# Crossings of the second block done token tile by token tile

## The chip, the cores and the metric

One core of one Trainium2 chip runs the whole program. The metric is the device time of one execution in microseconds (us); three executions of the kernel before are given, and one more was recorded by the hardware profiler. Engines: PE is TensorE, DVE VectorE, ACT ScalarE, POOL GpSimd, SP SyncE (it issues DMAs).

## What is computed

Two transformer blocks follow each other, each of two layers, on 256 tokens of 1024 features in float32. The change touches the second block (layers 2 and 3 of the program). Cut to what matters there:

```
for each layer of block 2:
    g1, s1, gate1, g2, s2, gate2 = rows and columns of c @ w_ada + b_ada
    h = rmsnorm(x) * (1 + g1) * g_attn + s1          # 256 x 1024
    q, k, v of three kinds of attention = h @ w_in   # 13 weight tiles
    y = attention(...)                               # 256 x 1024
    x = x + gate1 * (y @ w_out)                      # 4 weight tiles
    h = rmsnorm(x) * (1 + g2) * g_ffn + s2
    layer 2:  x = x + gate2 * ((silu(h @ w_gate) * (h @ w_up)) @ w_down)   # 11 steps of 256 hidden columns
    layer 3:  a router picks 2 of 8 experts for each token; x = x + gate2 * their sum
```

## The kernel before

Tokens are two tiles of 128 (`TT = 2`, index `t`), features eight chunks of 128 (`KC = 8`, index `k`), output columns two halves of 512 (index `c`). All large products are made of three: weights and left sides are each split in a high part (`w_hi`, `hT_hi`, rounded by ACT) and a low part (`w_lo`, `hT_lo`, the rest, by DVE or POOL), and `product` (L2379 to L2383) multiplies high by high, high by low and low by high. So every weight tile of 128 x 2048 goes through: DMA into a raw slot of `slab` (SP, L648), the high part on ACT (`hi`, L1920, about 1.9 us), the low part on DVE (`lo`, L999, 2.29 us) or on POOL in four pieces (L848), and products on PE. `Tiles` numbers the tiles and their raw and split slots, and `POOLED` says which low parts POOL makes. PE waits for a low part in `next_low`, and releases a split slot with `w_used`. Every engine works through its own program in order; the order of tiles and waits is written out by hand.

A *crossing* is what lies between the last products of a stage and the first of the next. In block 2 there are four: into layer 2 from block 1 (whose last layer ends with the modulation's rows, L2820), from layer 2's output tiles to its gated stage, from its down tiles to layer 3, and from layer 3's output tiles to the router. The last three are `cross_gated` (L1098 on): DVE adds the four parts (c, t) to `x`, gated (`add_gated`, L1095 and L1096), in the order (0,0), (0,1), (1,0), (1,1); ACT squares each half row (`square_halves`, L1951), DVE makes the mean (L1105, L1110), POOL the root (`norm_roots`, L828), DVE scales the row into `h` (L1118). PE turns all 16 chunks (`turn_rows`, L2392), with `tp_done` raised only at token tile 1. `turn` then takes the chunks one by one, 256 tokens wide: DVE applies gain and shift out of PSUM into `htf` (L1039), ACT rounds to `hT_hi` (L1985), DVE takes the rest to `hT_lo` (L1034). PE waits with `rows_one` for each chunk and uses it for both token tiles at once.

Around the crossings: `out_tile(2, FA)` does both token tiles of output half 0, then `out_last` half 1. POOL makes the low parts of the first two gate/up tiles, and roots between their pieces (`ff_lo`); SP loads the next gate/up tile only after both (`pool_lo(FF0[l] + 1)`). In a gated step ACT does silu (L2247) and then the high parts of the next tiles; DVE does the gate product (L598), then low parts, then the hidden low part (L1587); PE turns the hidden rows (`turn_step`, L2500). The last step is `down` for the tile before the last, with `turn_step(J - 1)` in its middle, then `down_last`. In layers 2 and 3 POOL makes tile 2's low part (`lo_of(l, 2)`) and ACT its high part before the turning (`hi_of(l, 2, 3)`). In layer 3 the router's products (`wr_hi`) take each chunk of `hT`, then PE turns all of `htf` for the rows that are gathered, and DVE copies the logits out (`lgT`, L1693).

## Time and profile before

| what | value |
| --- | --- |
| device time, median of 3 runs (lowest, highest) | 1903.46 us (1903.06, 1904.87) |
| profiled execution, its time | 1903.16 us |
| profiled execution, its span | 1901.4 us |
| PE busy | 1812.2 us, 95% |
| DVE busy | 1413.7 us, 74% |
| ACT busy | 1115.0 us, 59% |
| POOL busy | 385.0 us, 20% |
| mean granted PE clock | 0.981 |

All times in the rows are us from the start of the span. A row of a timeline has the start, the duration, the engine, the line, the operation with its output and inputs, the number of merged instructions, and in brackets how long the engine stood idle before it and what released it. The busy time of PE is modelled from its matmuls, which overlap, so 95% does not mean that it multiplies at its peak. The granted clock of 1.00 is 2.4 GHz, of 0.50 1.2 GHz.

### The profile page before, as it was taken

Reading aid. Unit: us, or ns where it says so; the run is one execution under the profiler, and the core shown is the slowest. Engines: PE = TensorE matmul, PEld = TensorE weight load, DVE = VectorE, ACT = ScalarE, POOL = GpSimd, SP = SyncE. Lnnn points to the kernel's source line nnn. Section 1 sums busy time; section 2 is a strip of 40 time slices with the busy share of each in tenths; the row PEclk is TensorE's granted clock in tenths of the full one; section 3 lists DMA queues with packets and bytes.
Section 4 is the critical chain, followed back from the end, with each engine's and each line's share of the span. In section 5 each row is a group of like instructions: output and inputs, shape, how many; then the busy total and the mean of one; then the engine's idle time right before and its main releaser. Section 6 shows DMA issues by size and latency. Waiting matters only on the chain.

```text
span 1901.4 us, 25928 instructions
## 1 busy us (share of the span) xinstructions
PE 1812.2 (95%) x8751; PEld 1476.9 (78%) x8751; DVE 1413.7 (74%) x1655; ACT 1115.0 (59%) x1296; POOL 385.0 (20%) x315
## 2 busy tenths in 40 slices
PE   7899999989999998899989789999999999999997
PEld 6678886868888786688878568888888888888885
DVE  5748874466976486645457759888988888889897
ACT  6745444564444454443345537777777777777775
POOL 3732213462211373200046400000000000000000
PEclk9999999999999998999989989999999999999999
DMA  8348884418987341455544249999999999999994
GB/s 271 111 167 330 333 348 149 143 58 302 361 331 290 105 156 45 155 189 186 193 155 144 100 178 352 384 378 386 376 384 381 380 381 380 380 377 382 384 381 166
DMA packets 237934, 506.39 MB, mean 266 GB/s; under 512 B 23304, under 2 KB 74720, under 8 KB 231712
## 3 DMA queue, kind: packets, MB, share of 16 engines
q1 hardware_dynamic: 225664, 492.85, 71.2%
q0 software_dynamic: 3008, 10.32, 2.0%
q10 hardware_dynamic: 9184, 2.23, 0.5%
q8 instruction: 43, 0.70, 0.2%
q14 instruction: 35, 0.29, 0.0%
HBM read 497.42 MB, written 7.91 MB: 266 GB/s over the span
## 4 chain that ended last, share of the span: by engine, by line
PE 83%; issue 6%; DVE 5%; ACT 4%; POOL 1%; DMA 0%; POOLq 0%; SPq 0%; DVEq 0%; ACTq 0%
PE bank L2381 26%; PE bank L2383 25%; PE bank L2382 25%; PE bank L2500 2%; ACT slab L2070 1%; ACT w_hi L1920 1%; PE bank L2820 1%; DVE slab L1317 1%; PE bank L2592 1%; PE bank L2569 1%; POOL w_lo L848 1%; PE bank L2551 0%; PE bank L2537 0%; DVE x L1096 0%; PE bank L2603 0%
## 5 line engine op out<-in xcount | busy, mean ns | idle before, releaser
L999 DVE TENSOR_TENSOR w_lo<-slab,w_hi 128x2048 fp32r<-128x2048 f32 x369 | 848.0, 2309 | 213.1 <-ACT w_hi L1920 212.5
L1920 ACT ACTIVATE w_hi<-slab 128x2048 fp32r<-128x2048 f32 (+2 forms) x421 | 796.6, 1899 | 326.3 <-PE bank L2383 251.5
L2381 PE MATMUL bank<-w_hi,hT_hi 128*128 128x512 f32 (+3 forms) x1664 | 648.7, 390 | 15.3 <-DVE hT_lo L1048 4.5
L2382 PE MATMUL bank<-w_lo,hT_hi 128*128 128x512 f32 (+3 forms) x1664 | 637.5, 383 | 0.0
L2383 PE MATMUL bank<-w_hi,hT_lo 128*128 128x512 f32 (+3 forms) x1664 | 637.5, 383 | 0.0
L2381 PEld LDWEIGHTS bank<-w_hi,hT_hi 128*128 128x128 f32 x1664 | 315.7, 190 | 77.3 <-DVE w_lo L999 8.8
L2383 PEld LDWEIGHTS bank<-w_hi,hT_lo 128*128 128x128 f32 x1664 | 315.3, 189 | 59.5
L2382 PEld LDWEIGHTS bank<-w_lo,hT_hi 128*128 128x128 f32 x1664 | 316.0, 190 | 55.2
L848 POOL TENSOR_TENSOR w_lo<-slab,w_hi 128x512 fp32r<-128x512 f32 (+2 forms) x208 | 256.0, 1268 | 375.7 <-ACT w_hi L1920 358.8
L2381 PE MATMUL bank<-w_hi,hid_hi 128*128 128x512 f32 x680 | 265.6, 391 | 0.7 <-DVE w_lo L999 0.7
L2383 PE MATMUL bank<-w_hi,hid_lo 128*128 128x512 f32 x680 | 264.9, 390 | 0.0
L2382 PE MATMUL bank<-w_lo,hid_hi 128*128 128x512 f32 x680 | 264.6, 389 | 0.0
L2381 PEld LDWEIGHTS bank<-w_hi,hid_hi 128*128 128x128 f32 x680 | 127.7, 188 | 29.3 <-issue 2.3
L2383 PEld LDWEIGHTS bank<-w_hi,hid_lo 128*128 128x128 f32 x680 | 127.6, 188 | 26.7
L2382 PEld LDWEIGHTS bank<-w_lo,hid_hi 128*128 128x128 f32 x680 | 127.7, 188 | 26.1
L946 POOL DMA_INDIRECT y_rows<-slab,posi x7 | 16.5, 2363 | 515.6 <-ACT slab L2293 515.6
L923 POOL TENSOR_TENSOR slab<-slab 128x512 f32<-128x512 f32 x32 | 58.9, 1858 | 252.8 <-ACT slab L2218 252.8
L1605 DVE SCALAR_TENSOR_TENSOR big<-slab,csilu,big 128x2048 f32<-128x2048 f32 x42 | 103.5, 2473 | 0.0
L2070 ACT ACTIVATE slab<-slab,att 128x256 f32<-128x256 f32 (+1 forms) x144 | 67.1, 469 | 48.8 <-DVE att L1293 39.7
L2209 ACT ACTIVATE hid_hi<-bank 128x512 fp32r<-128x512 f32 (+1 forms) x95 | 47.6, 528 | 46.1 <-PE bank L2500 46.1
L1587 DVE TENSOR_TENSOR hid_lo<-bank,hid_hi 128x512 fp32r<-128x512 f32 (+1 forms) x95 | 55.3, 603 | 0.0
L2569 PE MATMUL bank<-const,slab 128*128 128x128 f32 x224 | 35.7, 298 | 19.7 <-DVE slab L1317 13.1
(253 smaller groups left out, 1199.7 us busy)
## 6 DMA issues: line engine op xcount, KB each, us to landing
slab<-in_w_exp_gate SPq DMA_DIRECT2D x176, 512.0 KB, 7.0
slab<-in_w_exp_up SPq DMA_DIRECT2D x176, 512.0 KB, 7.4
slab<-in_w_exp_down SPq DMA_DIRECT2D x176, 512.0 KB, 7.0
slab<-in_w_ada SPq DMA_DIRECT2D x48, 1024.0 KB, 6.1
slab<-in_w_mlp_in SPq DMA_DIRECT2D x64, 512.0 KB, 6.2
slab<-in_w_mlp_out SPq DMA_DIRECT2D x64, 512.0 KB, 9.0
slab<-in_w_in SPq DMA_DIRECT2D x56, 512.0 KB, 5.1
slab<-in_w_out SPq DMA_DIRECT2D x32, 512.0 KB, 4.6
```

The costliest lines, as they stand in the source:

```text
L848: ins = pool.tensor_tensor(w_lo[:, q, o], raw(s)[:, o], w_hi[:, q, o].bitcast(F32), ALU.subtract)
L923: pool.tensor_tensor(scr(X_ACT2 + t * F_UP, F_UP), a, a, ALU.mult).then_inc(sq_done, 1)
L999: dve.tensor_tensor(w_lo[:, q, 0:n], raw(s)[:, 0:n], w_hi[:, q, 0:n].bitcast(F32), ALU.subtract).then_inc(lo_dve, 1)
L1587: dve.tensor_tensor(to_lo[:, f0:f0 + n, o], src, to_hi[:, f0:f0 + n, o].bitcast(F32), ALU.subtract).then_inc(hidl_done, 1)
L1605: ins = dve.scalar_tensor_tensor(acc, w, c, acc, ALU.mult, ALU.add)
L1920: act.activation(w_hi[:, q, 0:n], raw(s)[:, 0:n], ACT.Copy).then_inc(hi_done, 1)
L2070: act.activation(p, p, ACT.Exp, bias=att[:, 1, j, t:t + 1], scale=-1.0, accum_out=att[:, 2, j, t:t + 1]).then_inc(ex_done, 1)
L2209: act.activation(to_hi[:, f0:f0 + n, t * P:(t + 1) * P], src, ACT.Copy).then_inc(hidh_done, 1)
L2381: pe.matmul(dst, a_hi, b_hi, start=start, stop=False)
L2382: pe.matmul(dst, a_hi, b_lo, start=False, stop=False)
L2383: return pe.matmul(dst, a_lo, b_hi, start=False, stop=stop_)
L2569: ins = pe.transpose(bank[PT[s]][:, o:o + P], sp_row(l, s, u, t)[:, k * P:(k + 1) * P], ident)
```

## The change

In block 2 all work at the crossings is ordered by token tile. `cross_gated` adds (0,0), (1,0), (0,1), (1,1) as (c, t); ACT, not DVE, scales a row; `turn(t, b)` treats half the chunks of one token tile: four 128-column evacuations on DVE, then ACT's and DVE's parts for two chunks at a time. With `late`, DVE adds (1,1) before turning token tile 0, else after its first half. PE's new routines `out_by_token`, `in_tiles_by_token`, `up_by_token`, `next_up` and `down_by_token` hold two weight tiles and go through token tile 0 first, with `turn_row` of a token tile placed inside. The modulation gains of a layer (`mod_gains`) are computed ahead of the crossing. POOL makes its roots after both `ff_lo`. Tile 2's low part moves from POOL to DVE (`BY_DVE2`). In layer 3 ACT's `hi_of(l, 2, 3)` comes after `cross_gated`. The split slots of the gated stage start at 3, those of layer 3's tiles at 2, so that the first two gate/up tiles need not wait for the last output tiles. The gated stage's first silu is done per token tile. The diff, cut to its core:

```diff
@@ constants
+FF_SLOT, LAST_SLOT = 3, 2
-        BY_DVE1, BY_DVE2 = range(2, 6), range(3, 5)
+        BY_DVE1, BY_DVE2 = range(2, 6), range(2, 5)
-        ATT2_BANKS, FF2_BANKS = (6, 7, 2, 3), (2, 3, 4, 5)
+        ATT2_BANKS, FF2_BANKS = {DEPTH: (1, 2, 3, 7), DEPTH + 1: (0, 1, 2, 3)}, (2, 3, 4, 6)
@@ POOL
                     norm_roots()
-                    lo_of(l, 2)
                     lo_of(l, 5, 6, 7, 8, 9, 10, 11, 12, 13, 14)
...
                     if l < MOE:
-                        ff_lo(l, 0, norm_roots)
+                        ff_lo(l, 0)
                         ff_lo(l, 1)
-                    else:
-                        norm_roots()
+                    norm_roots()
@@ DVE
+            def turn(t, b, l, which):
+
+                m, o, at = turn_at(l, which), slice(t * P, (t + 1) * P), pairs_turned(l, which, t, b)
+                dve.wait_ge(tp_done, turns_before(m) + 2 * t + b + 1)
+                for i in range(2):
+                    for k in range(4 * b + 2 * i, 4 * b + 2 * i + 2):
+                        ins = dve.tensor_scalar(htf[:, k, o], turned_row(l, which, k, t), turn_gain(l, which, k), turn_shift(l, which, k),
+                                                ALU.mult, ALU.add)
+                    ins.then_inc(tpe_done, 1)
+                for i in range(2):
+                    ks = slice(4 * b + 2 * i, 4 * b + 2 * i + 2)
+                    dve.wait_ge(hh_done, splits_before(2 * DEPTH) + at + i + 1)
+                    dve.tensor_tensor(hT_lo[:, ks, o], htf[:, ks, o], hT_hi[:, ks, o].bitcast(F32), ALU.subtract).then_inc(hl_done, 1)
...
                 add(0, 0)
+                first_half(0)
+                add(1, 0)
+                mean(0)
                 add(0, 1)
...
                 if late:
                     add(1, 1)
+                    first_half(1)
+                    turn(0, 0, l, which)
                     mean(1)
+                    turn(0, 1, l, which)
                 else:
+                    first_half(1)
+                    turn(0, 0, l, which)
                     add(1, 1)
+                    turn(0, 1, l, which)
                     mean(1)
+                turn(1, 0, l, which)
+                turn(1, 1, l, which)
...
-                    cross_gated(add_last, l < MOE)
+                    cross_gated(add_last, l == MOE, l, 1)
@@ ACT
+            def cross_gated(late, l, which):
+
+                square_part(0, 0)
+                square_part(1, 0)
+                scaled_row(0, l, which)
+                square_part(0, 1)
+                turn(0, 0, l, which)
+                if late:
+                    square_part(1, 1)
+                    turn(0, 1, l, which)
+                else:
+                    turn(0, 1, l, which)
+                    square_part(1, 1)
+                scaled_row(1, l, which)
+                turn(1, 0, l, which)
+                turn(1, 1, l, which)
...
                 elif l > DEPTH:
-                    square_halves()
+                    cross_gated(True, l, 0)
                     hi_of(l, 2, 3)
-                    turn()
...
                     hi()
-                    if l == MOE:
-                        hi()
+                    hi()
@@ PE
+                def out_by_token():
+
+                    q = [next_low(), next_low()]
+                    for t in range(TT):
+                        for c in range(2):
+                            for k in range(4):
+                                if t and c and k == 2:
+                                    turn_row(0, l, 1)
...
+                def in_tiles_by_token():
...
+                        if not t and l > DEPTH:
+                            turn_row(1, l, 0)
...
+                    def up_by_token():
...
+                                if not t and k == 6:
+                                    turn_row(1, l, 1)
...
+                    def next_up():
+
+                        q = next_low()
+                        for t in range(TT):
+                            pe.wait_ge(sq_done, ub + t + 1)
+                            if t:
+                                turn_step(0)
...
+                    def down_by_token(at):
+
+                        pe.wait_ge(hidl_done, at + TT)
+                        before_last, last = next_low(), next_low()
...
+                        part(0, 0, before_last, False)
+                        part(0, 1, before_last, False)
+                        turn_step(J - 1)
+                        part(1, 0, before_last, False)
+                        pe.wait_ge(hidl_done, at + 2 * TT)
+                        part(0, 0, last, True).then_inc(part_done, 1)
+                        part(0, 1, last, True).then_inc(part_done, 1)
+                        part(1, 1, before_last, False).then_inc(w_used, 1)
+                        part(1, 0, last, True).then_inc(part_done, 1)
+                        part(1, 1, last, True).then_inc(w_used, 1)
+                        turn_row(0, l + 1, 0)
...
                 for t in range(TT):
+                    if t:
+                        turn_row(1, l, 1)
+                    for k in range(KC):
+                        if k % 2 == 0:
+                            split_pair(l, 1, t, k)
+                        ins = product(bank[5][0:NE, t * P:(t + 1) * P], wr_hi[:, k, :], wr_lo[:, k, :], *lhs(k, t), k == 0, k == KC - 1)
+                    if t:
+                        ins.then_inc(lgt_done, 1)
                     for k in range(KC):
                         ins = pe.transpose(bank[2 * t + k // 4][:, (k % 4) * P:(k % 4 + 1) * P], htf[:, k, t * P:(t + 1) * P], ident)
```

## Rows read from the trace of the kernel before

**Rows 1.** Stretches, gated loop: busy us (count) of PE, PEld, DVE, ACT, POOL; clock.

```profile
800.00:950.00 150.00, 150.00 (x680) 124.16 (x679) 74.03 (x63) 59.62 (x62) 0.00 (x0) 1.00 0.59 193
```

**Rows 2.** PE's timeline, layer 2's output tiles to gated stage: start, duration, idle before.

```profile
772.46 1.09 PE L2392 MATMUL bank<-const,h 128*128 128x128 f32 x8 [3.59 <-DVE h L1118]
...
777.39 0.77 PE L2381 MATMUL bank<-w_hi,hT_hi 128*128 128x512 f32 x1 [0.77 <-DVE hT_lo L1034]
...
777.95 0.63 PE L2382 MATMUL bank<-w_lo,hT_hi 128*128 128x512 f32 x1
...
778.38 0.63 PE L2383 MATMUL bank<-w_hi,hT_lo 128*128 128x512 f32 x1
...
791.15 0.77 PE L2500 MATMUL bank<-const,slab 128*128 128x128 f32 x4 [0.93 <-DVE slab L598]
```

**Rows 3.** Timeline of DVE, the same crossing.

```profile
763.54 0.69 DVE L1095 TENSOR_TENSOR slab<-bank,rowg 128x512 f32<-128x512 f32 x1 [10.33 <-PE bank L2383]
...
764.27 0.69 DVE L1096 TENSOR_TENSOR x<-slab,x 128x512 f32<-128x512 f32 x1
...
777.17 0.53 DVE L1039 TENSOR_SCALAR slab<-bank,modg,modcol 128x256 f32<-128x256 f32 x1
...
777.62 1.03 DVE L1034 TENSOR_TENSOR hT_lo<-slab,hT_hi 128x256 fp32r<-128x256 f32 x1
...
781.24 0.41 DVE L1034 TENSOR_TENSOR hT_lo<-slab,hT_hi 128x256 fp32r<-128x256 f32 x1
```

**Rows 4.** Timelines of ACT and POOL, the same crossing.

```profile
765.36 0.61 ACT L1951 ACTIVATE h<-x 128x512 f32<-128x512 f32 x1
...
770.95 0.54 POOL L828 TENSOR_TENSOR stat<-stat,half 128x1 f32<-128x1 f32 x1 [0.75 <-DVE stat L1110]
```

**Rows 5.** Groups by form (count, busy us, mean ns); ACT's timeline entering layer 2.

```profile
L1293 DVE CUSTOM_DVE_ANT_0 slab<-bank,const 128x256 f32<-128x256 f32 x60 | 23.3, 417 | 28.0 <-PE bank L2551 28.0
...
L1293 DVE CUSTOM_DVE_ANT_0 slab<-bank,const 128x128 f32<-128x128 f32 x28 | 8.0, 285 | 4.6 <-PE bank L2551 4.5
...
631.65 1.06 ACT L1942 ACTIVATE h<-x 128x1024 f32<-128x1024 f32 x1
```

**Rows 6.** Timelines of POOL and SP's queue, same crossing.

```profile
772.78 7.01 POOL L848 TENSOR_TENSOR w_lo<-slab,w_hi 128x512 fp32r<-128x512 f32 x5
...
780.13 0.38 SPq L648 DMA_DIRECT2D slab<-in_w_ff_gate  x1
```

**Rows 7.** Timelines of ACT and DVE at layer 2's last gated step.

```profile
954.11 0.66 ACT L2247 ACTIVATE slab<-bank 128x256 f32<-128x256 f32 x2 [8.91 <-PE bank L2383]
...
954.66 1.92 ACT L1920 ACTIVATE w_hi<-slab 128x2048 fp32r<-128x2048 f32 x1
...
956.61 2.29 DVE L999 TENSOR_TENSOR w_lo<-slab,w_hi 128x2048 fp32r<-128x2048 f32 x1 [1.33 <-ACT w_hi L1920]
```

**Rows 8.** Timelines of PE and ACT, down tiles of layer 2 to layer 3.

```profile
969.42 2.82 PE L2392 MATMUL bank<-const,h 128*128 128x128 f32 x12 [3.96 <-DVE h L1118]
...
968.37 3.69 ACT L1920 ACTIVATE w_hi<-slab 128x2048 fp32r<-128x2048 f32 x2
...
983.93 0.78 ACT L2047 ACTIVATE big<-bank 128x324 f32<-128x324 f32 x2 [4.02 <-PE bank L2383]
```

**Rows 9.** Stretches with the granted clock behind POOL's columns, same crossing.

```profile
968.00:970.00 2.00, 0.58 (x3) 0.58 (x4) 1.07 (x3) 2.00 (x3) 1.43 (x2) 0.67 1.08 358
...
978.00:980.00 2.00, 2.00 (x12) 2.00 (x12) 1.84 (x6) 1.17 (x3) 0.00 (x0) 0.77 0.67 251
```

**Rows 10.** Timelines of PE and POOL, entering layer 2.

```profile
647.38 0.40 PE L2381 MATMUL bank<-w_hi,hT_hi 128*128 128x512 f32 x1
...
634.68 5.02 POOL L848 TENSOR_TENSOR w_lo<-slab,w_hi 128x512 fp32r<-128x512 f32 x4 [0.60 <-ACT w_hi L1920]
```

**Rows 11.** Timelines of PE and DVE, layer 3's output tiles to router.

```profile
1108.06 1.47 PE L2392 MATMUL bank<-const,h 128*128 128x128 f32 x8 [2.17 <-DVE h L1118]
...
1117.90 0.41 DVE L1693 COPY slab<-bank 8x256 f32<-8x256 f32 x1 [0.61 <-PE bank L2383]
```

More of the change, by code:

```diff
@@ L169, in before_split @@
         if not self.looping and self.i - self.at < self.split:
-            return self.last.get(self.base + self.i % self.split)
+            return self.last.get(self.slot(self.i))
         return self.t - self.split
@@ L461, in splits_before, with turns_before, turn_at @@
             return 4 * min(m, 2 * DEPTH) + KC * max(0, m - 2 * DEPTH)
+        def turns_before(m):
+            return KC * min(m, 2 * DEPTH) + 4 * max(0, m - 2 * DEPTH)
+        def turn_at(l, which):
+            return 2 * DEPTH + 2 * (l - DEPTH) + which
+        PART0 = {l: PARTS * l if l < DEPTH else PARTS * DEPTH + 5 * (l - DEPTH) for l in LAYERS}
         def att_slot(k):
@@ L755, in _ @@
                     ff_end = ring.t
-                    ring.stage(RAW)
+                    ring.stage(RAW, base=LAST_SLOT)
                 else:
@@ L1243, in _ @@
                     norm()
+                    mod_gains(0)
+                    for t in range(TT):
+                        turn(t, 0, l, 0)
+                        turn(t, 1, l, 0)
                     ada_rows(l - 1)
[L1245 to L1250 removed]
                 if l == 0:
@@ L2795, in read_by_act @@
                         pe.wait_ge(act_done, ub + t + 1)
-                    up(rows_to, left, TT, COL, mlp_rows if l < DEPTH else rows_one)
+                    def up_by_token():
+                        q = []
+                        for t in range(TT):
+                            for k in range(KC):
+                                a, s = k // 4, slice(k % 4 * COL, (k % 4 + 1) * COL)
+                                if k % 4 == 0:
+                                    if not t:
+                                        q.append(next_low())
+                                if k % 2 == 0:
+                                    split_pair(l, 1, t, k)
+                                if not t and k == 6:
+                                    turn_row(1, l, 1)
+                                ins = product(rows_to[t][:, :], *lhs(k, t), w_hi[:, q[a], s], w_lo[:, q[a], s], k == 0, k == KC - 1)
+                                if t and k % 4 == 3:
+                                    ins.then_inc(w_used, 1)
+                            if not t:
+                                ins.then_inc(row_half, 1)
@@ new lines, in down_by_token, with part @@
+                    def down_by_token(at):
+                        pe.wait_ge(hidl_done, at + TT)
+                        before_last, last = next_low(), next_low()
+                        def part(t, c, q, spare):
+                            o = slice(t * P, (t + 1) * P)
+                            for f in range(2):
+                                s = slice(f * D + c * COL, f * D + (c + 1) * COL)
+                                f_hi, f_lo = hidden(f, ROWS_SPARE if spare else None)
+                                ins = product(sums_at(t, c), f_hi[:, o], f_lo[:, o], w_hi[:, q, s], w_lo[:, q, s], False, spare and f == 1)
+                            return ins
+                        part(0, 0, before_last, False)
[9 more added lines that the diff above has]
+                        turn_row(0, l + 1, 0)
```

240 lines of the change are left out of this document (126 added, 114 removed).

## The prediction

> **What bounds the kernel now.** Read first the page, where TensorE (PE) has by far the most busy time, then the table of stretches: in the gated loop of layer 2 PE is busy for all 150.00 us with 680 matmuls, 0.221 us each [rows 1]. A delay or gain before such a loop reaches the end undiminished. What this change can touch are PE's holes at the four crossings of block 2, so the timelines there come next, PE's first (a hole shows as "idle before"), then VectorE's (DVE), ScalarE's (ACT) and GpSimd's (POOL) for what fills it. I call them X1 (into layer 2), X2 (its output tiles to its gated stage), X3 (its down tiles to layer 3), X4 (layer 3's output tiles to the router).
>
> At X2 PE stops at 772.46 - 3.59 = 768.87, turns token tile 0, waits, turns tile 1, waits 0.77, and multiplies from 777.39 at a pitch of 0.43 (777.95 to 778.38) instead of 0.22; its first hidden transposes come at 791.15 [rows 2]. Meanwhile DVE works almost without a break [rows 3].
>
> **Prices.** A gated addition is two DVE instructions of 0.69, 1.34 in all; evacuating one 256-column chunk starts 0.45 before the next instruction (777.17 to 777.62); a low part is 0.41, but 1.03 while POOL splits weights [rows 3]. The square of half a row is 0.61, some 0.8 with the read of its sum, and POOL's root 0.54 [rows 4]. The halved evacuation (128 columns, two pointer scalars) isn't in the trace. The masked maximum takes 0.417 for 256 and 0.285 for 128 columns [rows 5], so 128 columns are worth 0.13: 0.45 - 0.13 = 0.32 a piece. The bound from below is the 0.285 row less the overlap of 0.08 (0.53 - 0.45), 0.21; from above 0.45. I take 0.32, since it is the same operation with its width alone changed. One token-and-half group `turn(t, b)` is then 4 x 0.32 + 0.1 + the wait for ACT's second high part + 2 x 0.38, about 2.2; four of them 8.8, against 8 x (0.45 + 0.34) = 6.3 for today's eight chunks. Scaling a row goes from DVE to ACT, where 1024 columns took 1.06 [rows 5]. Today's chunk of 256 columns takes 0.53 from start to end [rows 3]. The Trainium skill (VectorE: DVE Perf Modes, the section on the TRN2 errata) gives an instruction from PSUM 120 cycles fixed and one per element, an estimate of 0.39 for the chunk and 0.26 for a piece; the trace does not agree, and the measurement decides. By the page's figure a group is about 0.25 shorter and each crossing 1 us; the sum would come out some 3 lower.
>
> **X2, the gain.** Output tiles 2 and 3 are four sets of 12 matmuls, 2.7 each. They started at 768.87 - 10.9 = 758.0 and end sets at 760.7, 763.4, 766.2 (and 768.9). Tile 0's additions now come after the first two, so: add 760.8 to 762.2, square to 763.0, add 763.5 to 765.0, square 765.8, mean 766.05, root 766.7, row scaled by ACT 767.9. PE wants it at 767.5 inside its last set: 0.4 idle. Transposes (1.0) and rest end 770.4. DVE is held by `first_half(1)`, whose square is behind the row scaling on ACT, to 768.9; group (0,0) ends 771.1, its first pair is ready at 770.8. DVE then adds the last part (to 772.5) and does group (0,1): pair 2 at 774.3, PE idle 0.8. PE then needs token tile 1 turned after pair 2, at 775.7. Its row is behind ACT's last high part (774.35), the square (775.2), mean, root (776.1) and scaling (777.2): 1.6 idle. From 777.3 PE has the 8 transposes, 6 matmuls, 24 for token tile 1: 785.1. The second pair of gate/up tiles is loaded earlier: POOL's two splits no longer end at 779.8 (772.78 + 7.01), which is what SyncE waited for before loading at 780.13 [rows 6], but at 765, as both use free slots. Its high part still stands behind ACT's turns (to 781.8): high 783.7, low 786.1, gate product 786.5: PE waits 1.4, then ends those tiles at 786.5 + 10.9 + 0.5 = 797.9. Before: 791.15 + 0.77 + 10.9 = 802.8. **Gain 4.9.** The slow low parts (1.03 against 0.41) go with POOL's splits. If PE's clock falls in these holes, half a slow stretch, up to 3.4, is lost again: bounds 1.5 to 5.5.
>
> **X3, a loss.** `down_by_token` takes both split tiles before its first product: `before_last, last = next_low(), next_low()`. Before, PE needed only the earlier one at this point. The last down tile's split stands behind the last gate step: silu 954.11, high part from 954.66, low part 956.61 to 958.90 [rows 7]. PE is ready at 953.9 and would wait to 958.9: **5.0 idle** where 12 matmuls ran. The rest of the 48 matmuls and the four transposes is as long as before, so the down tiles end at 970.4, not 965.46 (969.42 - 3.96 [rows 8]). All DVE, ACT and POOL work behind is later too. Chain from the first finished part: add 965.1 to 966.5, square, add to 969.0, square, mean 970.05, root, scale 971.9; transposes; additions of tile 1 hold DVE to 972.9; groups (0,0) to 975.1; the second square of tile 1 stands before ACT's next high parts, so mean 975.9, (0,1) to 977.9; row 1 scaled by 978.7; PE turns it at 979.3 to 980.3; (1,0) to 982.0, (1,1) to 984.1. Then comes the next one: `hi_of(l, 2, 3)` moves behind ACT's turns. Before, it ran at 968.37 in the hole [rows 8]. And tile 2's low part moves from POOL to DVE, behind its turns. High part 983.9 to 985.8, low 988.1. PE waits there, where it went straight on at 983.9 (ACT reads the finished tiles at 983.93 [rows 8]). **Loss 4.2** at a full clock. But today's 3.96 idle was followed by a granted clock of 0.67 in 968 to 970, then the lower level (1.2 GHz), until 0.77 in 978 to 980 [rows 9], which puts the slow stretch at 968.7 to 978.9. A 5.0 idle should do the same over 957 to 964: 5 us of half speed in the down tiles, 2.5 later, of which 2.3 reach the chain. **Loss 6.5**, bounds 2.4 (cheap pieces, clock kept) to 9 (a second slow stretch in tiles 0 and 1).
>
> **X1, a small loss.** The transposes start as before, behind other PE work. The first pair is ready 1 us earlier, but DVE's four groups take 8.8: 637.3 to 646.1, then `ada_rows` 0.65, then tile 2's low part 2.3: 649.1. PE began tile 2 at 647.38, as POOL had made this low part by 634.68 + 5.02 [rows 10]. **Loss 1.8**, bounds 0 (cheap pieces) to 2.5.
>
> **X4, a loss.** PE stopped at 1105.9 (1108.06 - 2.17); the logits left it for DVE's copy at 1117.90 [rows 11]. After: parts at 1097.8, 1100.5, 1103.2; row 0 scaled 1104.9; transposes push the last set to 1107.25. Here `late` is true: DVE's last addition waits for it before any turning, to 1108.7. Groups (0,0) to 1111.0; ACT's square after its high parts, mean 1111.7; (0,1) to 1113.8; row 1 scaled 1114.6. PE: router products to 1114.4, eight transposes of `htf` at the slow pitch of X3's (2.82 for 12, so 0.23 each [rows 8]) to 1116.2, only then `turn_row(1)`. Four are done at 1117.1: (1,0) to 1119.4, (1,1) to 1121.5, logits copied at about 1121.5 to 1122. The other copies on ACT end before the selection needs them. **Loss 3.6**, bounds 1.5 to 4.5.
>
> **Sum.** 1.8 - 4.9 + 6.5 + 3.6 = +7.0 us. The profiled execution took 1903.16 (span 1901.4); the median shown is 1903.46, 0.3 above. 1903.46 + 7.0 = 1910.5.
>
> **The rivals.**
> - *Pieces are cheap (not slower).* At a pitch of 0.21 each group of four is 0.45 shorter, 1.8 in each of X1, X3, X4 and 0.5 in X2: +7.0 - 5.9 = +1.1, 1904.6. For: the 0.285 row. Against: today's chunk takes 0.53 where that operation takes 0.417. At 0.27 it is about +4 still; below that it decides. 0.17. The Trainium skill's figure above (VectorE: DVE Perf Modes, an estimate of 0.26 a piece from start to end) lies on this side.
> - *The clock holds.* No slow stretch in X3 (-2.3) and X4 (-1.4): +3.3, 1906.8. For: 0.93 idle at 791.15 was followed by no slow matmuls. Against: 5.0 is longer than the 3.59 and 3.96 that were [rows 2, 8]. 0.17.
> - *Overlap everywhere.* If each crossing gave X2's 4.9, X3's waits being covered (another order on DVE than the code has), and X1 nothing: about -14, 1889. Against: DVE's unbroken work. 0.08.
> - *Clock falls in X2 as well and twice in X3*: +3.4 + 2.5 and 1 in X1: +14, 1917. 0.10.
>
> **How the numbers follow.** My case 0.48. Range 1900.5 to 1916.5: cheap pieces with the clock kept below, most of the last rival above, leaving out overlap everywhere. A measurement here tells about 0.2% (3.8 us) from no change. Faster 0.10 (overlap 0.08, tail of cheap pieces); same 0.27 (cheap pieces 0.14, clock 0.10, 0.03 of mine); slower 0.63.
>
> **What would show it.** X2: PE's hole of 3.59 gone, the table load and silu at about 785, hidden transposes at about 789. X3: PE idle about 5 ended by DVE's low part ahead of the first down product; a second hole ended by a low part ahead of tile 2; the span of 12 matmuls slow after it. X1: DVE's split between `ada_rows` and tile 2's products. X4: `lgT` copied 3 to 4 later after PE's last output matmul. DVE's 128-column evacuations at 0.40 long. Wrong if the down tiles start at once, or if pieces are near 0.28.

## The result and the profile after

The changed kernel is slower than the kernel before, by more than was forecast and beyond the range.

| what | before | after |
| --- | --- | --- |
| device time, median | 1903.65 us (4 runs) | 1922.28 us (4 runs, 1921.09 to 1923.44) |
| ratio, 95% interval | | 1.0098 (1.0086 to 1.0110) |
| profiled execution: time, span | 1903.16, 1901.4 us | 1921.96, 1919.8 us |
| mean granted PE clock | 0.981 | 0.978 |

The page of the kernel after, its busy times: PE does 5.6 us more in 18.4 us more span, so most of the loss is waiting.

```profile
PE 1817.8 (95%) x8775; PEld 1481.0 (77%) x8775; DVE 1423.2 (74%) x1683; ACT 1121.3 (58%) x1302; POOL 377.0 (20%) x307
```

**Where it is.** I took the same PE instruction in both traces at seven places and subtracted the two distances between neighbouring places. Predicted terms stand beside what came out (us, after less before; at the last place after is 18.7 behind, the sum but for rounding):

| stretch | predicted | measured |
| --- | --- | --- |
| the program's start to the first transposes of layer 2 (code untouched) | 0 | +1.3 |
| X1, and on to 700 us | +1.8 | +2.7 |
| attention of layer 2 | 0 | +0.4 |
| X2 | -4.9 | -4.0 |
| X3 | +6.5 | +10.6 |
| attention of layer 3 | 0 | +0.2 |
| X4, to the first expert's products | +3.6 | +7.6 |

PE's timeline of after at X2. It answers to [rows 2]: the hole of 3.59 is one of 1.45, the eight transposes of the second row take 1.06 at a full clock, and ahead of the next gate/up pair PE waits 1.14 for DVE (1.4 forecast).

```profile
773.34 1.09 PE L2439 MATMUL bank<-const,h 128*128 128x128 f32 x8 [1.45 <-ACT h L2012]
...
782.26 1.06 PE L2439 MATMUL bank<-const,h 128*128 128x128 f32 x8 [1.15 <-ACT h L2012]
...
791.55 0.47 PE L2430 MATMUL bank<-w_hi,hT_hi 128*128 128x512 f32 x1 [1.14 <-DVE slab L629]
```

A part of X2's gain may be PE's clock. Before has a stretch at the lower level over its transposes and first products here, and after has none. Two stretches of the same kind as in [rows 1], first of before, then of after:

```profile
774.00:781.00 7.00, 5.58 (x17) 4.47 (x18) 6.18 (x11) 2.08 (x5) 5.79 (x5) 0.51 0.01 2
```

```profile
773.00:781.00 8.00, 7.01 (x32) 5.10 (x32) 5.82 (x16) 3.21 (x10) 0.54 (x1) 1.00 0.99 348
```

How much of the gain the new order would bring by itself, at the same clock, no run tells.

DVE's timeline of after at X1. Four pieces take 1.36 to 1.37, and groups follow each other in 2.19 (640.89 to 643.08): 0.32 a piece and 2.2 a group, as priced. Behind them stands tile 2's low part, at 648.05, and PE's first product of tile 2 comes at 650.38, against 647.38 before [rows 10]; 1.26 of that was there before X1. The rest of X1's +2.7, 0.9, comes between tile 2 and 700 us.

```profile
640.89 1.36 DVE L1060 TENSOR_SCALAR slab<-bank,modg,modcol 128x128 f32<-128x128 f32 x4
...
643.08 1.36 DVE L1060 TENSOR_SCALAR slab<-bank,modg,modcol 128x128 f32<-128x128 f32 x4
...
648.05 4.47 DVE L1026 TENSOR_TENSOR w_lo<-slab,w_hi 128x2048 fp32r<-128x2048 f32 x2
```

PE's timeline of after at X3, to be read beside [rows 8]. The first line is the hole of `next_low()` ahead of the down tiles (5.0 forecast); the last is tile 2, 2.20 behind DVE's low part. Between them PE turns the second row at 984.14.

```profile
959.39 0.72 PE L2430 MATMUL bank<-w_hi,hid_hi 128*128 128x512 f32 x1 [4.96 <-DVE w_lo L1026]
...
975.54 1.09 PE L2439 MATMUL bank<-const,h 128*128 128x128 f32 x8 [2.91 <-ACT h L2012]
...
978.17 0.61 PE L2430 MATMUL bank<-w_hi,hT_hi 128*128 128x324 f32 x1 [1.53 <-DVE hT_lo L1066]
...
984.14 1.04 PE L2439 MATMUL bank<-const,h 128*128 128x128 f32 x8
...
992.97 0.50 PE L2430 MATMUL bank<-w_hi,hT_hi 128*128 128x512 f32 x1 [2.20 <-DVE w_lo L1026]
```

Stretches of after (busy us and counts of PE, PEld, DVE, ACT, POOL, then the granted clock, DMA share, GB/s). Three fall in X3, behind its holes: the first behind 4.96, the second behind 2.91 and 1.53, the third behind 2.20. One of over 20 us covers X4's second half and most of the gather. Before, X3 had one at 968 to 979 [rows 9].

```profile
959.00:964.00 5.00, 4.61 (x14) 3.68 (x15) 0.25 (x1) 0.00 (x0) 0.00 (x0) 0.66 0.73 245
976.00:984.00 8.00, 6.47 (x30) 6.26 (x29) 4.52 (x14) 3.43 (x9) 0.54 (x1) 0.57 0.19 70
993.00:997.00 4.00, 4.00 (x11) 3.15 (x12) 3.90 (x7) 3.21 (x3) 0.71 (x1) 0.57 0.74 228
1124.00:1146.00 22.00, 16.33 (x92) 15.01 (x93) 13.59 (x40) 5.54 (x12) 0.06 (x1) 0.50 0.41 152
```

PE's and then DVE's timeline of after at X4. PE has holes of 3.31 and 1.48; then the eight transposes of `htf` (L2977) and only then the second row (L2439), each 1.91 at the lower level; DVE waits 3.52 for that row. The gather takes 6.40, in before 5.44. The logits are copied 15.9 later than before [rows 11], 4.8 of it new since the entry of X4.

```profile
1121.73 0.23 PE L2430 MATMUL bank<-hT_hi,wr_hi 128*8 128x128 f32 x1 [3.31 <-DVE hT_lo L1066]
...
1124.31 0.27 PE L2430 MATMUL bank<-hT_hi,wr_hi 128*8 128x128 f32 x1 [1.48 <-DVE hT_lo L1066]
...
1125.55 1.91 PE L2977 MATMUL bank<-const,slab 128*128 128x128 f32 x8
...
1127.26 1.91 PE L2439 MATMUL bank<-const,h 128*128 128x128 f32 x8
...
1141.75 6.40 PE L2997 MATMUL bank<-slab,h 128*128 128x128 f32 x32 [1.37 <-DVE slab L1744]
```

```profile
1128.35 1.37 DVE L1060 TENSOR_SCALAR slab<-bank,modg,modcol 128x128 f32<-128x128 f32 x4 [3.52 <-PE bank L2439]
...
1133.78 0.41 DVE L1709 COPY slab<-bank 8x256 f32<-8x256 f32 x1 [0.97 <-PE bank L2432]
```

### The profile page after: what moved, and what is told of

Same layout as the page of the kernel before. It is cut to its first block, busy times and chain, and to the rows that moved or that the text cites. A ratio compares the mean times of both kernels' runs of the same rounds, so it can differ in the third digit from the quotient of the medians.

```text
span 1919.8 us, 26002 instructions
## 1 busy us (share of the span) xinstructions
PE 1817.8 (95%) x8775; PEld 1481.0 (77%) x8775; DVE 1423.2 (74%) x1683; ACT 1121.3 (58%) x1302; POOL 377.0 (20%) x307
## 4 chain that ended last, share of the span: by engine, by line
PE 80%; DVE 6%; issue 6%; ACT 5%; POOL 1%; DMA 1%; SPq 0%; POOLq 0%; DVEq 0%; ACTq 0%
PE bank L2430 24%; PE bank L2432 24%; PE bank L2431 24%; PE bank L2546 2%; ACT w_hi L1936 1%; ACT slab L2116 1%; PE bank L2959 1%; DVE slab L1060 1%; DVE slab L1335 1%; POOL w_lo L877 1%; PE bank L2639 1%; DVE w_lo L1026 1%; PE bank L2616 1%; DMA slab<-in_w_router 1%; PE bank L2598 0%
## 5 line engine op out<-in xcount | busy, mean ns | idle before, releaser
L877 POOL TENSOR_TENSOR w_lo<-slab,w_hi 128x512 fp32r<-128x512 f32 (+2 forms) x200 | 247.4, 1272 | 383.7 <-ACT w_hi L1936 366.8
```

Of the source, the lines that this page charges most:

```text
L877: ins = pool.tensor_tensor(w_lo[:, q, o], raw(s)[:, o], w_hi[:, q, o].bitcast(F32), ALU.subtract)
```

## The experiments

My theory was that the four crossings carry all of the loss, each by its own holes and by the slow clock (the lower level, 1.2 GHz) behind them. The rivals were a cost in what the change alters outside the crossings, and a shift that sets the stages against each other. Behind each time stand its ratio to the kernel before, measured beside it on the same chip, and the 95% interval; 0.001 is 1.9 us. "By the ratios" compares two kernels by these, which is fairer than their times where they ran on different chips.

**One crossing at a time.** For each crossing the order of before was put behind a switch: whole rows on DVE, ACT and PE, the old order of additions, the old output and down tiles. `WHOLE` lists (0, 0), (0, 1), (1, 0), (1, 1) for X1 to X4.

```diff
+WHOLE = {(0, 0), (0, 1), (1, 0), (1, 1)}
...
-                    cross_gated(add_last, l == MOE, l, 1)
+                    if whole(l, 1):
+                        cross_whole(add_last, l < MOE, l, 1)
+                    else:
+                        cross_gated(add_last, l == MOE, l, 1)
```

All four whole: 

> The changed kernel with all four crossings put back into the whole-row manner of before; kept of the change are the slot numbering of the weight tiles, tile 2's low part on VectorE, the gains worked out ahead, and the order of the roots on GpSimd. If the added time is all in the four crossings (my theory), this is before within 1.5 us: 1903 to 1905. If a part of it sits in what is kept (rival: tile 2's low part on VectorE and the slot order), it is 1906 or more. The start of the second block (first transposes, 636.67 before, 637.93 after) should be 636.7 if the 1.3 us of block 1 come from the crossings' code and 637.9 if they come from what is kept or from how things happen to fall.

Measured 1905.86 (1.0011, 1.0000 to 1.0023), between theory and rival. The first transposes of layer 2 come at 635.98 here and at 637.99 with X2 alone, so the 1.3 us of block 1 follow neither the crossings' code nor what is kept: they vary from one execution to the next. The first transposes of X2 come at 780.90, 10.42 idle, against 772.46 in before [rows 2], since POOL splits two gate/up tiles ahead of the roots that a whole-row X2 waits for, and the second waits for ScalarE. POOL's timeline of it:

```profile
774.64 4.92 POOL L892 TENSOR_TENSOR w_lo<-slab,w_hi 128x512 fp32r<-128x512 f32 x4 [13.37 <-ACT w_hi L2018]
779.52 1.36 POOL L874 TENSOR_TENSOR stat<-stat,half 128x1 f32<-128x1 f32 x2
```

So it is no clean zero: this order belongs to X2, and costs nothing only where X2 goes by token tile. With before's order of the roots:

```diff
-                        ff_lo(l, 0)
+                        ff_lo(l, 0, norm_roots if whole(l, 1) else None)
```

> As the kernel with all four crossings whole, with X2's roots on GpSimd put ahead of the last quarter of the first gated tile's low part, as before has them. The trace of the first such kernel shows its X2 transposes 6.2 us later than before's, behind the two low parts on GpSimd. Theory: that order is the whole of what it lost in X2, about 5 us, and what is left of the change outside its crossings (slots, tile 2's low part on VectorE) costs under 1.5 us: with the clock's stretch in X3 short (3.4 us, as in that kernel) 1899 to 1902, with before's long one (10.2 us) 1902 to 1905. Rival: the kept part costs something of its own: 1906 or more.

Measured 1900.91 (0.9988, 0.9979 to 0.9997), as the theory had it. On balance nothing outside the crossings costs anything: it gains 2.3 us by the ratio. The trace shows 0.8 lost in X1, where tile 2's low part is now on VectorE, and X3 2.7 shorter than in before. VectorE's low parts in it are no longer slowed by POOL splitting tile 2 beside them (first before, then this kernel), which is 1.1 by the next product, and the other 1.6 come while PE's clock is still low in before (10.2 us at the lower level there, 3.4 in this kernel).

```profile
972.96 1.48 DVE L1034 TENSOR_TENSOR hT_lo<-slab,hT_hi 128x256 fp32r<-128x256 f32 x1
```

```profile
972.89 0.42 DVE L1092 TENSOR_TENSOR hT_lo<-slab,hT_hi 128x256 fp32r<-128x256 f32 x1
```

This kernel, *all whole*, is the zero of the table below.

X2 alone: 

> Only X2 by token tile, the other three crossings whole. Theory: X2 alone gains what the trace of after shows between its ends, 4.0 us, and hands it on: about 1899.5 (1898.5 to 1901). Rival: the gain is taken back in the gated stage or in layer 3, then 1903 or more.

Measured 1898.68 (0.9970, 0.9957 to 0.9982): the theory.

X3 alone: 

> Only X3 by token tile. Theory: 8 to 9 us slower than the kernel without it (the trace of after has 8.6 between its ends, the prediction had 6.5), some 1911 to 1913, half of it in TensorE's 5 us hole ahead of the last down tiles and the rest at the lower clock level in the holes behind it. Rival: it costs only the 4.2 us of the first hole, since most of the slow clock was there before: 1908.

Measured 1918.16 (1.0073, 1.0060 to 1.0087), more than theory or rival.

X4 alone: 

> Only X4 by token tile. Theory: 4.9 us between its ends and 2.7 behind it, where gather and first expert run at the lower clock level in after: 1910 to 1911.5. Rival: what is behind it belongs to X3's shift and not to X4: 1908 to 1908.7, with the first expert's silu at most 5 us late.

Measured 1912.68 (1.0050, 1.0036 to 1.0063). X3 alone and X4 alone still have the late roots of the first kernel, so they are 0.0062 and 0.0039 over that one: 11.8 and 7.4 us. X4's 7.4 is the 7.6 of the theory, on a higher base. X3's 8 to 9 were too low: they were read against before, whose own X3 is 2.7 longer than the whole-row one kept here.

X1 put back: 

> The changed kernel with X1 alone put back. Theory: X1 is 1.5 to 2.5 us of the change (the piecewise order on VectorE ahead of layer 2's first tiles), so 1919.5 to 1921 against 1922.3 of after. Rival: X1 shifts attention of layer 2 against GpSimd's low parts and the 1.4 us added there are its work too: 1917 to 1919.

Measured 1920.32 (1.0083, 1.0069 to 1.0097), 2 us under after (2.9 by the ratios), with intervals that overlap. In the trace X1 is 2.0 shorter and the attention behind it 2.6 longer, so what X1 is worth at the end isn't settled.

What each kernel takes in a stretch over *all whole*, from the same PE instructions as above (us):

| kernel | X1 | attention 2 | X2 | X3 | X4 |
| --- | --- | --- | --- | --- | --- |
| before | -0.8 | 0.0 | +0.2 | +2.7 | 0.0 |
| after | +1.9 | +0.4 | -3.8 | +13.3 | +7.6 |
| X2 alone | 0.0 | +1.2 | -3.8 | +1.1 | +0.1 |
| X3 alone | -0.1 | +1.4 | (+4.5) | +13.1 | +0.1 |
| X4 alone | -0.1 | +1.4 | (+4.5) | 0.0 | +7.2 |
| X1 put back | -0.2 | +3.0 | -3.8 | +13.0 | +7.6 |
| late take | +2.0 | +0.9 | -3.8 | +7.1 | +7.6 |
| late take, early high parts | +2.3 | +0.5 | -3.8 | +3.8 | +7.3 |
| all edits | +1.9 | +0.5 | -3.8 | +3.7 | +3.5 |
| all edits, high parts split | +1.8 | +0.6 | -3.8 | +1.7 | +3.2 |

The crossings add up: each costs the same alone and together (X3 13.1 and 13.3, X4 7.2 and 7.6, X2 -3.8 in every kernel). That settles the rival of a shift for them; it isn't settled for X1 and the attention behind it, which goes from 0.4 to 3.0. The 4.5 in brackets are the late roots.

**X3's holes.** The late take:

```diff
-                        before_last, last = next_low(), next_low()
+                        before_last = next_low()
...
                         pe.wait_ge(hidl_done, at + 2 * TT)
+                        last = next_low()
                         part(0, 0, last, True).then_inc(part_done, 1)
```

> The changed kernel with one line moved: TensorE takes the last down tile (waits for its low part) only before its first product, no longer before those of the tile ahead of it. Theory: the 5.0 us hole ahead of the down tiles in X3 is that wait and nothing else, and one stretch at the lower clock goes with it (3.4 us of stretch, 1.5 of time): 1916 to 1918. Rival 1: the hole's time is only moved, TensorE waits later for the same low part or for the hidden rows: 1920 or more. Rival 2: the stretches at the lower clock are set by the later holes and stay: 1917.5 to 1918.5, clock stretches in X3 unchanged.

Measured 1916.17 (1.0062, 1.0048 to 1.0076), the theory: 6.1 under after (6.9 by the ratios), and 6.2 less between X3's ends. The hole is gone, and the slow stretch behind it:

```profile
952.00:960.00 8.00, 7.01 (x34) 5.48 (x33) 4.08 (x7) 5.46 (x7) 1.71 (x3) 1.00 0.08 12
```

Added to it, the early high parts:

```diff
                 scaled_row(1, l, which)
+                between()
                 turn(1, 0, l, which)
                 turn(1, 1, l, which)
...
-                    cross_gated(True, l, 0)
-                    hi_of(l, 2, 3)
+                    cross_gated(True, l, 0, lambda: hi_of(l, 2, 3))
```

> As the late take, and ScalarE makes the high parts of layer 3's tiles 2 and 3 right after the second scaled row, where it stands idle 3.8 us, no longer behind the last transposed pieces. Theory: the 2.2 us hole at tile 2 shrinks by the 1.6 us by which VectorE's low part waits for the high one, and its stretch at the lower clock (3.4) may go with it: 1.5 to 3.5 us below the late take. Rival: VectorE is what ends last there, and the pieces behind the high parts come later by as much: within 1 us of the late take.

Measured 1911.85 (1.0042, 1.0028 to 1.0056), 4.3 under the late take, more than the theory's 1.5 to 3.5: PE's wait ahead of tile 2 falls from 2.22 to 0.73, and the third slow stretch goes. So two orderings made 9.5 of X3's 13.3.

**X4: order and clock.** The second row first:

```diff
-                    if t:
-                        turn_row(1, l, 1)
                     for k in range(KC):
...
                     if t:
                         ins.then_inc(lgt_done, 1)
+                    else:
+                        turn_row(1, l, 1)
                     for k in range(KC):
                         ins = pe.transpose(bank[2 * t + k // 4][:, (k % 4) * P:(k % 4 + 1) * P], htf[:, k, t * P:(t + 1) * P], ident)
```

> Only X4 by token tile, and in it TensorE turns the second scaled row right behind the first token tile's router products, ahead of the eight transposes of the first tile's htf that stand there in the change. In the trace of X4 alone VectorE waits 3.52 us for that row's transposes, which TensorE issues only behind those eight (1.91 us at the lower clock level). Theory: this place in TensorE's order costs 1.7 us: 1910.5 to 1911.5 against 1912.7. Rival: what counts is the sum on TensorE up to the gather, the order inside it is all the same: within 0.5 us of 1912.7.

Measured 1910.01 (1.0038, 1.0023 to 1.0053), 2.3 under X4 alone by the ratios. In the trace X4 gets 3.7 shorter, more than the 1.7 of the order, and it spends less time at the lower clock level: 17.1 us from 1112 to 1140, against 23.9 from 1114 to 1145 in X4 alone.

The clock, by transposes of a constant in PE's two holes:

```diff
                     for k in range(KC):
+                        for _ in range({0: 26, 4: 10}.get(k, 0) if not t else 0):
+                            pe.transpose(bank[0][:, 0:P], ident, ident)
                         if k % 2 == 0:
                             split_pair(l, 1, t, k)
```

> Only X4 by token tile, and TensorE fills its 3.3 us hole ahead of the first router products with 26 transposes of the identity into a bank that is free, and the 1.5 us hole ahead of the fifth with 10; their results are used by nothing. They need 2.8 and 1.1 us at full clock, so they end before what they wait for. Theory: the lower clock comes from these holes, so the stretch at 1114 to 1121 goes or comes later, and the time falls by 1.7 to 3.5 us: 1909 to 1911. If the longer stretch of 1124 to 1139 goes with it, up to 6: 1906.5. Rival: the stretches are not set by these holes: 1912.2 to 1914, the fillers at most 0.5 us in the way.

Measured 1908.98 (1.0032, 1.0021 to 1.0044), 3.4 under X4 alone by the ratios, 3.5 shorter in the trace: the theory. First X4 alone, then the kernel with fillers, the same stretch:

```profile
1114.00:1121.00 7.00, 4.88 (x29) 4.41 (x28) 3.33 (x11) 2.34 (x5) 1.25 (x2) 0.51 0.56 225
```

```profile
1114.00:1121.00 7.00, 4.83 (x49) 3.78 (x47) 4.77 (x16) 2.96 (x6) 1.10 (x2) 1.00 0.56 225
```

PE's timeline of the kernel with fillers: 26 transposes fill the hole to 0.47, and the eight transposes behind take 1.04, not 1.91.

```profile
1109.30 3.00 PE L3112 MATMUL bank<-const 128*128 128x128 f32 x26
...
1112.77 0.23 PE L2530 MATMUL bank<-hT_hi,wr_hi 128*8 128x128 f32 x1 [0.47 <-DVE hT_lo L1081]
...
1116.29 1.04 PE L3119 MATMUL bank<-const,slab 128*128 128x128 f32 x8
...
1117.16 1.04 PE L2539 MATMUL bank<-const,h 128*128 128x128 f32 x8
```

No other edit was made, so PE's clock falls here by the crossing's own holes, and half of X4's loss (3.5 of 7.2) went with the fillers. Not all slow time went: of 23.9 us at the lower level from 1114 on in X4 alone 10.2 are left, from 1127 to 1141, over the gather and the first expert. The Trainium skill (TensorE: Matmul & The Clock Gate, the section on HAM oscillation) describes a matmul kernel in which each wait is followed by work at the lower clock; these rows agree, in that filling the waits takes the lower clock away from the transposes behind them.

Both edits (with 9 transposes in the second hole): 

> Only X4 by token tile, with both edits: the second row turned first and the fillers in the holes. Alone they gave 2.7 and 3.7 us of X4's 7.4. Theory: the first works largely through the transposes at the lower clock level, so they overlap by about 1 us: 5 to 5.8 us together, 1907 to 1907.7. Rival: they add up, 1906.2 or less; or the fillers do all of it, 1909.

Measured 1908.38 (1.0023, 1.0013 to 1.0033), 5.1 under X4 alone by the ratios, 4.1 in the trace. They overlap more than the theory had it, in the trace by 3.0 of 7.1: each takes away the same slow transposes. What is left of X4 in the trace, 3.1 us, was not taken apart.

**What is left of X3.** TensorE's order first:

```diff
+                                if not t and l > DEPTH and k0 + k == 6:
+                                    turn_row(1, l, 0)
...
-                        if not t and l > DEPTH:
-                            turn_row(1, l, 0)
```

> The late take and early high parts, and in layer 3 TensorE turns the second scaled row ahead of the last two chunks of tile 1's products of the first token tile, no longer behind them. In the trace of those two edits VectorE waits 3.44 us for that row's transposes (976.3) though the row was scaled by 974.1. Theory: X3's remaining cost is this place in TensorE's order, as in X4: 1.5 to 2 us below the 1911.9 of the two edits, 1909.9 to 1910.4. Rival: VectorE's pieces, 8.8 us for both token tiles, bound X3 whatever TensorE's order: 1911.4 or more.

Measured 1911.91 (1.0037, 1.0023 to 1.0052): the rival. X3 is 0.4 shorter in the trace.

The clock; `filler(n, to)` issues n transposes of the identity into a bank that is free:

```diff
+                        filler(18, bank[3][:, 3 * P:4 * P])
                         turn_row(0, l + 1, 0)
...
                     q = []
+                    if l > DEPTH:
+                        filler(11, bank[3][:, 3 * P:4 * P])
```

> The late take and early high parts, with 18 transposes of the identity in TensorE's 2.1 us hole ahead of layer 3's first transposes and 11 in the 1.4 us hole behind them. Theory: the stretch at the lower clock at 968 to 976 (6.8 us) comes from these holes; with it gone 2 to 3.5 us below 1911.9: 1908.5 to 1910. If the shift also shortens the 13.6 us stretch in X4, 1906. Rival: the stretch is set by the products' own holes behind (1.4 and 1.5 us) or just moves: within 0.7 of 1911.9.

Measured 1910.30 (1.0033, 1.0022 to 1.0044), below the two edits alone by less than the intervals tell apart. Its trace decides against the theory: PE's clock stays up in 968 to 976 (0.57 there with the two edits alone), yet X3 is as long (3.7 against 3.8). PE only waits longer, 2.54 against 1.36, for VectorE, and behind this hole comes a new stretch at the lower level, 3.4 us from 980.6. Without it X3 could be only some 0.5 shorter: tile 2's low part, which VectorE makes behind its pieces, is ready at 985.12, and PE's first product of tile 2 comes at 985.65.

```profile
968.00:976.00 8.00, 6.89 (x53) 6.22 (x52) 6.85 (x18) 5.06 (x11) 1.00 (x2) 1.00 0.54 179
```

```profile
980.45 0.53 PE L2430 MATMUL bank<-w_hi,hT_hi 128*128 128x324 f32 x1 [2.54 <-DVE hT_lo L1066]
```

All edits together: 

> All four crossings by token tile, with every edit tried so far: late take, early high parts, earlier second row in X3 and X4, fillers in the holes of X3 and X4. Theory: they add up: 1911.9 less 1.8 (order in X3), 2.5 (fillers in X3), 2.7 (order in X4) and 3 (fillers in X4, part of it gone with the order) is 1902, within 0.2% of before: so what the change lost was in these places. Rival: they overlap, since each takes away the same stretches at the lower clock: 1905 or more.

Measured 1904.83 (1.0002, 0.9993 to 1.0011): no difference from before, though 2.8 above the sum of the theory. The loss of 18.6 us is gone, and X3 and X4 have 13.7 less of it by the table. That doesn't make these crossings free: they still cost 3.7 and 3.5 over all whole, which X2's -3.8 and the gain outside the crossings make up for. Nor are fillers a gain of this form alone, as the last kernel below shows. VectorE's timeline of it in X3, from the first piece to tile 2's low part, 12.3 us, with a wait of 1.82 for ScalarE's high parts; then the same two places in *all whole*, 6.7 apart:

```profile
968.14 1.37 DVE L1060 TENSOR_SCALAR slab<-bank,modg,modcol 128x128 f32<-128x128 f32 x4
...
977.53 0.76 DVE L1066 TENSOR_TENSOR hT_lo<-slab,hT_hi 128x256 fp32r<-128x256 f32 x2 [1.82 <-ACT hT_hi L2001]
...
980.39 4.49 DVE L1026 TENSOR_TENSOR w_lo<-slab,w_hi 128x2048 fp32r<-128x2048 f32 x2
```

```profile
971.87 1.00 DVE L1096 TENSOR_SCALAR slab<-bank,modg,modcol 128x256 f32<-128x256 f32 x2 [1.30 <-PE bank L2552]
...
978.54 4.49 DVE L1044 TENSOR_TENSOR w_lo<-slab,w_hi 128x2048 fp32r<-128x2048 f32 x2
```

With tile 3's high part behind the turns again:

```diff
-                    cross_gated(True, l, 0, lambda: hi_of(l, 2, 3))
+                    cross_gated(True, l, 0, lambda: hi_of(l, 2))
+                    hi_of(l, 3)
```

> The kernel with all edits, where in X3 ScalarE makes only tile 2's high part ahead of the last transposed pieces, and tile 3's behind them. In the trace of the kernel with all edits VectorE waits 1.82 us there for ScalarE, which spends 3.69 us on both high parts. Theory: VectorE's chain of pieces is what is left of X3 (3.4 to 3.8 us over the whole-row form), so the wait's 1.8 us come back: 1903 against 1904.8, X3's ends 1.6 to 1.9 us closer. Rival: TensorE's products of the first token tile are the bound, the wait is covered: within 0.4 us, with X3's ends unchanged.

Measured 1905.23 (1.0010, 1.0001 to 1.0019). The trace follows the theory: the wait is gone, tile 2's low part starts at 979.20, X3 is 2.1 shorter (1.7 left) and the span 2.3 shorter. A part of the 2.1 is the clock: a stretch of 3.4 us at the lower level, from 978.1, is gone too. With all edits tile 2's low part is ready at 982.68 and its first product comes at 983.21, 0.5 behind it; here at 981.48 and 981.53. So about 1.7 is VectorE's chain and 0.4 the clock. The median doesn't show it; single runs of these two kernels spread over 6.5 and 4.6 us. That VectorE's chain bounds what is left of X3 is read from the traces; a gain in the time isn't shown.

**Towards a faster kernel.** X2 alone with tile 2's low part back on POOL:

```diff
-        BY_DVE1, BY_DVE2 = range(2, 6), range(2, 5)
+        BY_DVE1, BY_DVE2 = range(2, 6), range(3, 5)
...
+                    lo_of(l, 2)
                     lo_of(l, 5, 6, 7, 8, 9, 10, 11, 12, 13, 14)
...
-                    pool_tiles(2)
-                lo(width_of(l, 2))
+                    pool_tiles(2 if l < DEPTH else 3)
+                if l < DEPTH:
+                    lo(width_of(l, 2))
```

> X2 alone by token tile, and the low part of tile 2 back on GpSimd in layers 2 and 3. The traces with all crossings whole show tile 2's first product 0.8 us later with the low part on VectorE, in layer 2. Theory: 0.8 us in each of the two layers comes back: 1896.5 to 1898 against 1898.7, and this is the fastest version. Rival: GpSimd's later low parts then hold back attention, as the added part stands ahead of tiles 5 to 14 there: 1899 or more.

Measured 1898.82 (0.9978, 0.9969 to 0.9988): 0.7 back in X1, but X3 is 2.7 over all whole, against 1.1 with X2 alone. VectorE's first two low parts in X3 take 1.55 and 1.04 again, beside POOL's split of tile 2, and 0.43 and 0.42 with X2 alone: this confirms what slowed them in before. No gain over X2 alone is shown.

X2 and X3: 

> X2 and X3 by token tile, with the late take of the last down tile and the early high parts in X3; X1 and X4 whole. In the kernel with all four crossings by token tile and these two edits X3's ends were 3.8 us farther apart than whole (2.7 at tile 2 of layer 3 against -1.0 ahead of the down tiles). Theory: X3 keeps costing that, so 1901 to 1903 against 1898.7 of X2 alone. Rival: without X1's and X4's shifts the clock's stretches fall elsewhere and X3 is even: 1898 to 1900.

Measured 1902.53 (0.9997, 0.9988 to 1.0006): the theory, X3 costs the same, 3.7.

X2 alone, tile 2's low part on POOL, and fillers in the whole-row X3 and X4 (34 and 18 in `turn_rows`, 13 behind X3's, 18 before the wait for `sel_done`):

```diff
+                filler({(1, 0): 34, (1, 1): 18}[(l - DEPTH, which)] if (l - DEPTH, which) != (0, 0) else 0, bank[0][:, 0:P])
                 for t in range(TT):
                     xns[0] += 1
                     pe.wait_ge(xn_done, xns[0])
...
```

> X2 alone by token tile, tile 2's low part on GpSimd, and fillers in the holes of the whole-row X3 and X4 (34 transposes ahead of X3's and 18 ahead of X4's, 13 behind X3's, 18 ahead of the router's places). Theory: of 20.5 us at the lower clock in X3 and X4 of the version without fillers some 10 go, each worth half of itself: 1893 to 1895 against 1898.8. Rival: most of those stretches lie where TensorE only waits, so they cost nothing: 1897.5 to 1899.5.

Measured 1897.42 (0.9961, 0.9947 to 0.9975), the lowest of all, though its interval overlaps those of the two kernels before it with X2 alone. In the trace X3 is 2.1 shorter by the fillers and X4 0.5 longer. The theory had 4 to 6; the time is 3.2 lower by the ratios, and 1.4 by the medians, at the edge of the rival's range. So the whole-row crossings pay for the clock too, about 2 us of it in X3 by the trace.

## Why the prediction was wrong

**The direction and the mechanisms stood; the sizes of X3 and X4 didn't.** In order:

- *Price of a piece*: right (0.32 pitch, 2.2 a group). The cheap-pieces rival is out. The Trainium skill's figure (VectorE: DVE Perf Modes, the section on the TRN2 errata) gave an estimate of 0.26 for a piece from start to end; the trace has 0.40.
- *X1*: 1.8 forecast (its own times, 649.1 less 647.38, make 1.7), and 1.7 measured at tile 2's first product, where the forecast ended. By 700 us the loss is 2.7. The 0.8 of all whole is in it, from tile 2's low part on VectorE. Where the 0.9 behind tile 2's first product comes from wasn't looked into.
- *X2*: 4.9 forecast, 4.0 measured, 3.8 over all whole in every kernel that has it. Alone it makes the kernel faster (0.9970), 3.4 under all whole by the ratios. As forecast, the slow stretch that before has there is gone too.
- *X3*: the step that failed is "5 us of half speed in the down tiles, 2.5 later", as the only slow stretch. The hole was 4.96 as forecast. But the holes of 2.91 and 1.53 behind it were followed by a second stretch (976 to 984) and the 2.20 at tile 2 by a third (993 to 997), where I had taken the old stretch as gone and none as new. Worked out as 4.2 at a full clock and 2.3 of clock, X3 was 10.6. One more stretch was in my text as a bound ("a second slow stretch"), which stopped at 9. X3's two orderings, which I named, were 6.2 and 3.3 with their clock; of the 3.8 left, 2.1 went with a shorter chain on VectorE.
- *X4*: 4.8 of loss at the logits against 3.6, with VectorE's steps within 0.2 of the forecast to the last group (1128.35, less the 11.1 by which X4 is entered late, is 1117.3; forecast 1117.1). The step that failed is that the sum ended there: I followed the chain to the copy of the logits and took what is behind as unchanged. There the gather took 6.40 for 5.44, with the clock at 0.50, and the products behind it were late as well, 2.8 in all. 3.5 of the 7.2 of X4 alone went with fillers. The 1.4 of clock that the rival "the clock holds" takes off X4 has no working; its only slow work, the eight transposes at 0.23, is worth 0.9 (1.91 against 1.06 in after).
- *The end*: of the distance of 11.6 between forecast and result, X3 has 4.1, X4 4.0, X2 0.9, X1 0.9, the attentions 0.6; 1.3 arose in block 1, where nothing was changed (by the traces; these make 11.8).
- *Clock falls in X2 as well and twice in X3* (0.10) came nearest, at 1917, partly by luck: more than one slow stretch in X3 was right, but X2's clock stayed up, and its price left out X4.

## What to carry to other kernels

When work is split finer at a place where TensorE waits, price each hole twice: once as waiting, once as slow work behind it, and follow the slow work on beyond the last instruction that the change touches. Take a tile in TensorE's order only where its first product stands, and put the work that another engine waits for ahead of work that nobody waits for: these two rules of order were worth 6 and, in X4 and for X3's high parts, 2 to 4 us here; in X3 the second gave nothing for the scaled row (0.4 in the trace), since VectorE's pieces ended last. Before a change is judged as a whole, put its parts behind switches; here one of four parts gained and two others hid it.

## What was not expected of the hardware

**Half the slow time is not always lost.** Taking away 6.8 us of slow stretch in X3, with 3.4 new behind it, gave 0.1 in the trace, since VectorE was the bound under it; in X4 the same step took away 13.7 and gave 3.5. The Trainium skill (TensorE: Matmul & The Clock Gate, the section on HAM oscillation) counts the penalty as half of the slow time; here both steps gave less. And the same work can meet a stretch or miss it: in attention of layer 2, which no experiment changed, the clock of all whole was back at 1.00 from 744, while with X2 alone the whole of 741 to 748 was slow, and with it more of the output products. First all whole, then X2 alone:

```profile
726.00:734.00 8.00, 6.67 (x34) 4.51 (x36) 7.04 (x30) 7.04 (x21) 0.12 (x1) 0.57 0.00 0
740.00:744.00 4.00, 4.00 (x17) 2.69 (x16) 3.77 (x14) 2.88 (x11) 4.00 (x4) 0.57 0.01 4
744.00:748.00 4.00, 4.00 (x20) 3.25 (x19) 1.29 (x3) 0.00 (x0) 0.61 (x1) 1.00 0.52 154
```

```profile
726.00:734.00 8.00, 4.30 (x36) 2.77 (x37) 7.23 (x35) 7.60 (x25) 1.64 (x1) 1.00 0.00 0
741.00:748.00 7.00, 6.36 (x21) 4.51 (x22) 5.92 (x17) 3.01 (x11) 5.46 (x5) 0.51 0.05 11
```

That is worth 1.2 us there, and up to 3.0 in the kernel with X1 put back. The start of the second block, with the same code in all kernels, lay between 635.5 and 641.7 in the profiled executions, so a difference of 1 to 2 us between two single traces must be read stretch by stretch, not from the spans.
